# Another order of copies, sums and weights in the seven-product stages of a two-block transformer kernel, its attention queries by halves and a part of its branch products inside the attention's tail

## The reference, cut to what matters

```python
h = _rmsnorm(x, norm1_g[l]) * (1.0 + scale1) + shift1
proj = h @ w_in[l]                                    # 1024 x 4352
qa, ka, va, qd, kd, vd, ga, gd = jnp.split(proj, points, axis=-1)
out_a = _sliding_window_attention(...)                # 8 heads, 512 wide
...
out_d = _diff_attention(...)                          # 4 heads of 128, then an RMS norm
merged = (jax.nn.sigmoid(ga) * (out_a @ w_branch_swa[l])
          + jax.nn.sigmoid(gd) * (out_d @ w_branch_diff[l]))
x = x + gate1 * (merged @ w_out[l])

h2 = _rmsnorm(x, norm2_g[l]) * (1.0 + scale2) + shift2
# _conv_ffn: u = h2 @ w_up (1024 x 5632), split into a and g
a = ap[:, 0:s] * conv_w[0] + ap[:, 1:s + 1] * conv_w[1] + ap[:, 2:s + 2] * conv_w[2] + conv_b
return (jax.nn.gelu(a, approximate=False) * g) @ w_down
```

## Time and profile before

| | before |
|---|---|
| median of 3 runs | 2781.86 us (2779.5 to 2788.24) |
| the profiled execution | 2779.05 us, span 2777.2 us |
| mean granted clock of PE | 0.974 of full speed |
| PE busy | 2594.6 us (93%), 12363 matmuls |
| DVE, ACT, POOL busy | 1548.2, 1110.3, 854.9 us (56, 40, 31%) |
| chain that ended last | PE 75%, DVE 12%, ACT 6%, DMA 4% |
| its largest lines | L1654 28%, L1739 21%, L1808 8% |
| a weight split of POOL, mean | 1030 ns (L1468) and 2431 ns (L1473) |

### The profile page before, as it was taken

One profiled execution on the slowest core, in us unless ns is written; L12 is line 12 of the kernel. 1 busy time (PEld: TensorE's weight loads), 2 busy tenths in 40 slices (PEclk: granted clock), 3 DMA queues, 4 the chain that ended last, 5 costly groups with the idle time before them and its releaser, 6 DMA issues.

```text
span 2777.2 us, 34668 instructions
## 1 busy us (share of the span) xinstructions
PE 2594.6 (93%) x12363; PEld 2157.6 (78%) x12363; DVE 1548.2 (56%) x2099; ACT 1110.3 (40%) x1866; POOL 854.9 (31%) x626
## 2 busy tenths in 40 slices
PE   3899999999999999999899988869997999999998
PEld 2688888788788799987788868757876888887887
DVE  5666665640325466657864428765568777772112
ACT  3400001421401588856544437660255555551000
POOL 1133332012233566620232220233102233225664
PEclk7999999999999999999999999999999999999999
DMA  5244443343266544435253347413242333338933
GB/s 216 80 148 137 137 143 115 100 161 133 84 215 194 141 107 107 107 125 159 91 184 113 116 119 191 175 39 122 76 145 68 114 106 107 118 96 303 294 90 123
DMA packets 375993, 374.81 MB, mean 135 GB/s; under 512 B 36068, under 2 KB 284301, under 8 KB 375693
## 3 DMA queue, kind: packets, MB, share of 16 engines
q1 hardware_dynamic: 345564, 303.90, 36.9%
q10 hardware_dynamic: 30256, 68.69, 6.6%
HBM read 286.55 MB, written 85.98 MB: 134 GB/s over the span
## 4 chain that ended last, share of the span: by engine, by line
PE 75%; DVE 12%; ACT 6%; DMA 4%; issue 1%; POOL 1%; SPq 0%; ACTq 0%; DVEq 0%; POOLq 0%
PE PS L1654 28%; PE PS L1739 21%; PE PS L1808 8%; PE PS L752 5%; PE PS L730 2%; PE PS L1721 2%; PE PS L1698 1%; DMA mod_raw<-in_w_ada 1%; PE PS L716 1%; PE PS L715 1%; DVE opBf L2847 1%; PE PS L1853 1%; ACT opA L1998 1%; ACT opBf L1994 1%; DVE M L2508 1%
## 5 line engine op out<-in xcount | busy, mean ns | idle before, releaser
L1654 PE MATMUL PS<-opA,w_hi 128*128 128x512 f32 x2304 | 722.1, 393 | 19.1 <-POOL w_lo L1473 13.7
L1654 PEld LDWEIGHTS PS<-opA,w_hi 128*128 128x128 f32 x2304 | 435.8, 189 | 113.5 <-POOL w_lo L1473 16.1
L1654 PE MATMUL PS<-opA,w_lo 128*128 128x512 f32 x1152 | 451.0, 391 | 0.0
L1468 POOL CAST w_hi<-w_raw 128x1024 fp32r<-128x1024 f32 (+1 forms) x120 | 123.6, 1030 | 776.1 <-PE PS L1654 467.4
L1739 PE MATMUL PS<-opB,Xr 128*128 128x512 f32 x1120 | 309.7, 394 | 15.0 <-ACT M L2173 15.0
L1473 POOL TENSOR_TENSOR w_lo<-w_raw,w_hi 128x1024 fp32r<-128x1024 f32 (+1 forms) x122 | 296.6, 2431 | 84.5 <-ACT w_hi L2053 74.9
L1739 PE MATMUL PS<-opA,Xr 128*128 128x512 f32 x980 | 278.7, 395 | 6.3 <-DVE M L2864 3.4
L2508 DVE SCALAR_TENSOR_TENSOR M<-mod_raw,small,M 128x512 f32<-128x512 f32 x168 | 176.0, 1048 | 162.3 <-DMA mod_raw<-in_w_ada 82.5
L1739 PEld LDWEIGHTS PS<-opB,Xr 128*128 128x128 f32 x1120 | 212.9, 190 | 61.2 <-ACT M L2173 16.3
L1654 PEld LDWEIGHTS PS<-opA,w_lo 128*128 128x128 f32 x1152 | 218.1, 189 | 45.1 <-issue 0.2
L1739 PEld LDWEIGHTS PS<-opA,Xr 128*128 128x128 f32 x980 | 184.1, 190 | 50.7 <-ACT M L2173 8.4
(11 more groups left out here) (241 smaller groups left out, 4687.8 us busy)
## 6 DMA issues: line engine op xcount, KB each, us to landing
mod_raw<-in_w_ada SPq DMA_DIRECT2D x96, 256.0 KB, 2.9
z_dram<-opB ACTq DMA_DIRECT2D x44, 512.0 KB, 3.9
w_raw<-in_a_w_in SPq DMA_DIRECT2D x32, 512.0 KB, 4.8
hin<-q_dram SPq DMA_DIRECT2D x64, 256.0 KB, 5.9
w_raw<-in_w_down SPq DMA_DIRECT2D x32, 512.0 KB, 4.3
opA<-z_dram SPq DMA_DIRECT2D x60, 256.0 KB, 5.1
mod_raw<-in_b_mod_w SPq DMA_DIRECT2D x48, 256.0 KB, 2.9
X<-x_dram SPq DMA_DIRECT2D x24, 512.0 KB, 7.5
```

Of the source, the lines that this page charges most:

```text
L1468: pool.tensor_copy(hi, raw).then_inc(pool_done, 1)
L1654: ins = pe.matmul(ps, w[:, k0 + k, :], rhs(part, k0 + k), start=(k == 0 and n == 0), stop=(k == chunks - 1 and n == 2))
```

## The change

It changes no arithmetic, and consists of three parts.

1. In the heads of both seven-product stages the first weights' copies come before the second half of the token copies, and the copies and sums come in another order. In the FFN yt gets a second tile (`yt_odd`), so that chunks take turns, and the first chunk's g half is copied out of PSUM (`first_gates`).
2. In the FFN's iterations both halves of chunk i + 1 are handled together, and `z_store` goes to the iteration's end.
3. In the second attention, queries of the first four chunks are loaded by halves of the tokens, the lower ones after P1 of the last in-projection iteration; the weights of branch units 0 and 1 are loaded and split inside the attention, and their 4 chunks that belong to the sliding-window half (48 matmuls) run inside its tail (`branch_swa`); the last norm has its own tile `d_last`, and its square stands one step sooner. Six of sixteen gate tiles are loaded later.

SP's list, for the queries, and PE's, for the branch products:

```diff
+            def query_half(c, e, hf):
+
+                t = slice(hf * HALF, (hf + 1) * HALF)
+                for part in range(2):
+                    sp.dma_start(opA[part * DH:(part + 1) * DH, e, c, t].bitcast(F32),
+                                 q2_dram[part, c * P + e * DH:c * P + (e + 1) * DH, t]).then_inc(q_half[c][hf], 16)
+                    step(q_half[c][hf], "q_half", c, hf, by=16)
...
             sp.wait_ge(in2_stored[1], at("in2_stored", U_IN2 + 17))
+            sp.wait_ge(pe_done, at("seven", U_IN2, LAST_IN2, P1))
+            for c in range(4):
+                for e in range(2):
+                    query_half(c, e, 0)
             sp.wait_ge(pe_done, at("seven", U_IN2, LAST_IN2, P7))
             sp.wait_ge(dve_done, at("seven_w", U_IN2, LAST_IN2, P3))
+            query_half(0, 0, 1)
             swa_keys_values(0)
+            sp.wait_ge(pe_done, at("seven", U_IN2, LAST_IN2, P4))
+            query_half(0, 1, 1)
+            for c in range(1, 4):
+                for e in range(2):
+                    query_half(c, e, 1)
 
             sp.wait_ge(pe_done, at("seven", U_IN2, LAST_IN2, P3))
-            for c in range(4):
-                queries(c)
-                if c == 1:
-                    swa_keys_values(1)
+            swa_keys_values(1)
             for j in range(DIFF_HEADS):
                 queries(4 + j)
             diff_keys(1)
```

```diff
+            def branch_swa(n, hf):
+
+                pe.wait_ge(pool_done, at("split", U_BRANCH + n))
+                if (n, hf) == (0, 0):
+                    pe.wait_ge(dve_done, at("swa_out", 3, 1))
+                    pe.wait_ge(dve_done, at("sec_p", STEPS - 1, 0))
+                for k in range(4):
+                    for m, (w, part) in enumerate(((0, 0), (1, 0), (0, 1))):
+                        pe.matmul(PS[:, 2 * n + hf, :], branch_part(n, w)[:, k, :], opA[:, part, k, hf * HALF:(hf + 1) * HALF],
+                                  start=(k == 0 and m == 0), stop=(k == 3 and m == 2))
+
+
             for t in range(SECOND_STEPS):
                 x = turned_at(t)
+                if x == 0:
+                    pe.wait_ge(dve_done, at("block", U_IN2, LAST_IN2, 0, 1))
+                if t == STEPS:
+                    branch_swa(0, 0)
+                if t == STEPS + DIFF_VALUE:
+                    branch_swa(0, 1)
                 if t < SWA_STEPS:
...
                     values(t)
+            for hf in range(2):
+                branch_swa(1, hf)
 
         def stick_act(act):
```

The loop of the FFN stage, ACT's list and then DVE's:

```diff
             for i in range(1, SEVENS[q]):
                 f = i + 2
                 snap(q, i, 0)
                 weight_high(q, i + 1, P1)
                 weight_high(q, i, P3)
-                gelu(f - 1, 1)
-                z_high(f - 1, 1)
+                if i == 1:
+                    for first in (1, 0):
+                        for hf in range(2):
+                            z_high(first, hf)
+                else:
+                    for hf in range(2):
+                        first_tap(f - 1, hf)
                 weight_high(q, i + 1, P2)
-                first_tap(f, 0)
-                z_store(f - 1)
                 snap(q, i, 1)
+                if i == 1:
+                    for hf in range(2):
+                        first_tap(f - 1, hf)
+                    z_store(0)
+                    z_store(1)
+                for hf in range(2):
+                    gelu(f - 1, hf)
                 weight_high(q, i + 1, P6)
-                gelu(f, 0)
                 weight_high(q, i + 1, P5)
+                if i > 1:
+                    for hf in range(2):
+                        z_high(f - 1, hf)
                 snap(q, i, 2)
                 weight_high(q, i + 1, P7)
                 weight_high(q, i + 1, P4)
-                z_high(f, 0)
-                first_tap(f, 1)
-            gelu(FC - 1, 1)
-            z_high(FC - 1, 1)
+                if i == 1:
+                    for hf in range(2):
+                        z_high(f - 1, hf)
+                z_store(f - 1)
+            for hf in range(2):
```

```diff
+            for i in range(1, SEVENS[q]):
                 f = i + 2
-                if i:
-                    other_taps(f - 1, 1)
-                    weight_low(q, i + 1, P1)
-                    weight_low(q, i, P3)
-                    gated(f - 1, 1)
-                    block_sum(q, i, 0, 0)
-                    z_low(f - 1, 1)
-                    weight_low(q, i + 1, P2)
-                    other_taps(f, 0)
-                    weight_low(q, i + 1, P6)
-                    weight_low(q, i + 1, P5)
-                    block_sum(q, i, 1, 1)
+                weight_low(q, i + 1, P1)
+                weight_low(q, i, P3)
+                for hf in range(2):
+                    other_taps(f - 1, hf)
+                block_sum(q, i, 0, 0)
+                weight_low(q, i + 1, P2)
+                for hf in range(2):
+                    gated(f - 1, hf)
+                weight_low(q, i + 1, P6)
+                weight_low(q, i + 1, P5)
+                for hf in range(2):
+                    z_low(f - 1, hf)
+                block_sum(q, i, 1, 1)
                 weight_low(q, i + 1, P7)
                 block_sum(q, i, 1, 0)
-                gated(f, 0)
                 weight_low(q, i + 1, P4)
```

More of the change, by code:

```diff
@@ L128 @@
 NO_UNIT = range(U_IN2 + 4, U_BRANCH)
+AHEAD = (U_BRANCH, U_BRANCH + 1)
+EARLY_GATES = [n for n in range(2 * KC) if n % KC < KC - 3]
+LATE_GATES = [n for n in range(2 * KC) if n % KC >= KC - 3]
+LAST_HALF = 2 * DIFF_HEADS - 1
 QK = 4
@@ L526, in program @@
         q_in = [sem(f"q_in{c}") for c in range(KC)]
+        q_half = [[sem(f"q_half{c}_{hf}") for hf in range(2)] for c in range(4)]
         k_in, v_in = [[sem(f"k_in{s}_{hf}") for hf in range(2)] for s in range(3)], [sem(f"v_in{s}") for s in range(2)]
@@ L666, in second_loads @@
                 sp.wait_ge(in2_stored[row], at("in2_stored", in2_unit(LAST_IN2, row)))
-            for n in range(2 * KC):
+            for n in range(2):
+                branch_weights(n)
+            for n in EARLY_GATES:
                 sp.dma_start(gates[:, n, :], gate_dram[n]).then_inc(gates_in, 16)
@@ L1027, in second_act @@
                     swa_high(y)
-                if half_at(t, 1) is not None:
-                    square(half_at(t, 1))
+                if squared_at(t) is not None:
+                    square(squared_at(t))
                 if half_at(t, RMS_LAG + 1) is not None:
@@ L1382, in _ @@
                         reload_half_spilled(U_IN2, j)
+                if u == U_BRANCH + 5:
+                    sp.wait_ge(pe_done, at("unit", U_BRANCH + 1, 1))
+                    for n in LATE_GATES:
+                        sp.dma_start(gates[:, n, :], gate_dram[n]).then_inc(gates_late, 16)
+                        step(gates_late, "gates_late", by=16)
                 if u in (U_IN2, U_FFN):
@@ L1639, in _ @@
                     second_pool()
-                if u not in SPLIT_BY_DVE and u not in NO_UNIT:
+                if u not in SPLIT_BY_DVE and u not in NO_UNIT and u not in AHEAD:
                     split(u)
@@ L1703, in quad @@
                                 step(pe_done, "unit", v, hf)
+                        if (first, hf, k) == (0, 1, QK - 1):
+                            ins.then_inc(pe_done, 1)
+                            step(pe_done, "b12_read", u)
                         if (first, hf, k) == (0, 0, 2):
@@ L2355, in first_copies, with first_gates @@
                 names[("free", u)] = names[("fa", f, 1)]
+            def first_gates(u):
+                for hf in range(2):
+                    act.wait_ge(pe_done, at("unit", u, 1))
+                    act.wait_ge(x_half[1], at("x_half", U_FFN, 1))
+                    act.wait_ge(dve_done, at("lo", "n2", 15))
+                    act.wait_ge(act_done, now(act_done))
+                    act.activation(first_gate(hf), PS[:, bank(u, hf), :], ACT.Copy).then_inc(act_done, 1)
+                    step(act_done, "first_gate", hf)
+                names[("free", u)] = names[("first_gate", 1)]
             def gelu(f, hf):
@@ L2360, in gelu @@
                 act.wait_ge(act_done, now(act_done))
[L2361 removed]
+                act.activation(gelu_tile(f, hf), gelu_tile(f, hf), ACT.Gelu).then_inc(act_done, 1)
                 step(act_done, "fg", f, hf)
@@ L3011, in _ @@
             weight_low(q, 0, P5)
+            weight_low(q, 0, P1)
+            weight_low(q, 0, P2)
             token_sums(q, 2)
+            token_sums(q, 3)
             weight_low(q, 0, P7)
             weight_low(q, 0, P3)
-            token_sums(q, 3)
-            weight_low(q, 0, P1)
-            weight_low(q, 0, P2)
+            for which in (P6, P5, P7, P4):
+                for c in range(QK):
+                    token_low(q, which, c)
             for hf in range(2):
                 other_taps(0, hf)
-            for c in range(QK):
-                token_low(q, P6, c)
-            for c in range(QK):
```

(11 more changed lines are left out.)

241 lines of the change are left out of this document (143 added, 98 removed).

## The result

The changed kernel takes 2805.94 us in the median of 4 runs (2801.18 to 2808.57), the kernel before beside it 2780.68. The medians are 25 us apart; the ratio is 1.0084, 95% interval 1.0059 to 1.0109, which makes it 23 us slower. The forecast was 2797, range 2766 to 2814.

The account below looks back on a forecast made before the run. PE, busy 2594.6 of 2777.2 us, was taken to bound the kernel. In-projection head −0.9, attention −23.0, FFN head +0.4, FFN loop +25.5 and clock +14 made +16: median 2797 us, range 2766 to 2814.

Parts of the forecast that it names:

- four taps in 4.2: Sign in the FFN loop: DVE's taps row at about 4.2 us in place of 3.2 for four.
- FFN head: FFN stage up to P1(2): old 11.28 us wait goes, some 14 us forms at P3(1); +0.4 us (−3 to +3).
- attention's start: Second attention up to its first turn: lower query halves asked for earlier shorten PE's 11.58 us idle; −6.7 us (−5 to −9).
- main case: 2.0 us stall at P3 each FFN iteration, clock falling behind about half: +16 us, 2788 to 2806; chance 0.45.
- FFN loop: FFN iterations 2 to 19: P3 waits for DVE's block_sum(1,1); 33.1 us of stalls less 7.6 saved, net +25.5 us.
- the two collisions: FFN loop: POOL sums delay DVE's taps and second z_low on the shared port; stall 2.0 us, a single collision 1.0.
- The clock: FFN loop: PE's clock drops behind half of 17 stalls, 1.7 us each; +14 us (0 to +29).
- The in-projection head: Up to the in-projection's first P3: PE begins sooner but DVE's list holds the same instructions; −0.9 us (−3 to +1.5).
- The splits inside the attention: Two POOL weight splits now stand inside its attention work; +1.5 us (0 to +3).
- The tail: Attention's end: 48 branch matmuls done in PE's waits, weights already split, 336 matmuls left in 76.2 us; −17.8 us.

Follow-up runs that it names:

- pool1: Changed kernel with POOL's weight sum for P5 alone held back until block_sum(1,1) in the FFN loop; 2779.02 us, ratio 0.9987.
- pool2: Changed kernel with POOL's weight sum for P3, and what is queued behind it, held back until block_sum(1,1) in the FFN loop; 2760.66 us, ratio 0.9921.
- head: pool2 with chunk 2's z_lows behind weight_low P4 in FFN iteration 1 alone; 2755.59 us, ratio 0.9900.
- allpieces: head with the branch splits' subtraction in eight pieces and every POOL weight sum of both seven-product stages in four; 2748.11 us, ratio 0.9862.
- keys: Kernel before with the attention's part alone, keys and values asked for ahead of the first two upper query DMAs; 2764.46 us, ratio 0.9936.

## Why the prediction was right, point by point

The mechanism was the forecast one, and its signs came: sixteen waits of nearly 2 us at P3, four taps in 4.2, one wait of 13.84 in the FFN head. One sign failed, on the attention's start. The size was short: 2806 lies at the upper end of the main case's own 2788 to 2806, and that the total isn't further off is in part luck, since errors in the loop had opposite signs.

- **The FFN loop** was the right place with the right price. The block sum was forecast at +17.60 to +18.29 and P3 at +18.34; that is where they are. Stalls: 33.1 us forecast for 17 of them. Measured, counted by P3's late start: 16 x 2.02 + 1.13 = 33.5. Two small things were missing. Iteration 19, which I had at 0, waits 1.30 (1.46 late), since the last chunk's work stands in it too. And each stall makes the twelve matmuls behind it 3.02 long in place of 2.88, 0.14 x 18 = 2.5 us. `pool1` and `pool2` show that the two collisions, not the count of DVE instructions, make the wait; the count costs 0.25 us an iteration.
- **The clock** was charged as half of 17 drops at 1.7, +14. It was 7 at 1.6, +11. The errors (2.5 + 1.5 against 3) cancel in large part, by luck. That drops follow some waits and not others of the same length I could not predict, and no run explains which.
- **The FFN head**: +0.4 forecast, +0.2 measured, with the wait of 13.84 us at P3(1) in place of 11.28 ahead of P6(1). `head` and `allpieces` confirm the reason, a backlog of DVE.
- **The in-projection head**: -0.9 forecast, -0.8 measured.
- **The attention's start** was mis-sized: -6.7 forecast, -3.7 measured (about -4.6 in eight of the eleven other kernels, -2.7 to -6.2 in all). The two waits there make 7.9 us, 3.7 less than the 11.58 of before and not the 5 to 9 less that were to show it. I had the first chunk's last upper query DMA issued at 1652.4. In the changed kernel, where this place lies 5.7 us later, that would be 1658.1. SP's timeline, and the two DMAs of that half (time of an issue in ns, then landing: least, median, most):

```profile
1641.17 11.91 SPq L684 DMA_DIRECT2D opA<-q_dram  x18
1653.12 3.02 SPq L638 DMA_DIRECT2D keys<-k_dram  x4
...
L684 SPq DMA_DIRECT2D opA<-q_dram x2: 969/2716/4463, 1657.6 to 1662.1; - x2
DMA to landing us min/median/max: 5.6/7.3/9.0
```

  The first was issued at 1657.6 and its issue took 4.46 us; so the second was issued only at 1662.1, landed 5.6 later, and PE's second wait ended at 1667.76, 3 us after the forecast place. I had also left out the keys' landing, which holds the first scores to 1663.0; but `keys` shows that their place in the queue doesn't matter, as the second wait takes over. Why that one issue took so long, no run shows.
- **The splits inside the attention** cost 3.2 where +1.5 was taken (range to +3). I priced them as POOL being late; they also hold DVE's short instructions, the same mechanism as in the loop, which I didn't apply there. The time at the lower clock in this stretch differs between executions: it takes 1.9 to 5.2 us more than before in the nine kernels with whole subtractions, and -0.2 to +1.8 in the three with pieces.
- **The tail**: -17.8 forecast, -16.4 measured, and here the forecast was better than this trace shows. In nine of the eleven other kernels the same stretch is 105.3 us in place of 107.0, which is -18.0. The difference is a clock drop at its start; PE has no further wait in it, and the branch row is the forecast one. Windows of the changed kernel and of `head` at the same place (granted clock is the number behind POOL's count), and the changed kernel's chain:

```profile
1855.60:1859.20 3.60, 3.52 (x13) 3.13 (x14) 1.04 (x4) 2.12 (x5) 0.51 (x1) 0.53 0.00 0
```

```profile
1853.00:1856.50 3.50, 3.46 (x28) 3.29 (x28) 1.98 (x6) 2.79 (x6) 0.47 (x1) 1.00 0.00 0
```

```profile
1880.72 76.17 PE PS L1754 x336
```

So +16 was 7 us short of +23, 6 of them in the attention: 3.0 at its start, 1.7 at the splits, 1.4 in a clock drop of the tail.

## What to carry to other kernels

A list that just fits its slot on paper has no room for what another engine takes from it: lay out the shared engine's instructions in time beside it, and count each pair of DVE and POOL instructions that both read two tiles in SBUF. Where such pairs can't be parted in time, cut POOL's instruction into pieces: POOL then takes longer and DVE loses next to nothing. That is a gain where a collision is on the path; where the pair had been parted already, the pieces cost 3.9 us in the loop of `allpieces`. When the profile of a change looks too bad or too good, cut both traces at the same instructions first; here 6 us of the difference lay in code that hadn't changed, and a stretch that loses 1.6 us to a clock drop in one execution doesn't in the next.

## What the runs showed of the hardware

- POOL's sum of 128 x 512 in one instruction beside four taps: POOL 1.30, taps 4.21. In four instructions: POOL 3.14, taps 3.36. DVE's loss falls from 1.03 to 0.18 us, though POOL works longer: the loss went with the length of one instruction of POOL, not with POOL's time in total.
- The Trainium skill, "SBUF — State Buffer", section "Who interferes with whom", calls the port pair that the two engines share an exclusive lock, and says that the order of issue decides who blocks. The trace agrees: POOL's sum at 2206.81 came 0.06 us ahead of the taps and delayed them, and the sum at 2216.02, which came 0.03 behind a low part of DVE, took 1.80 in place of 1.30.
- An idle time in a row is shorter than the delay: P3 started 2.02 us late where the row says 1.86, because the last matmul before it is counted for 0.39 us, where the start of the next one follows after 0.23. With the slower restart (3.02 us for twelve matmuls in place of 2.88) a stall shown as 1.86 costs 2.16, which is what P3 to P3 shows: 21.20 against 19.04.
- The clock fell behind 7 of the 16 waits of 1.86 to 1.88 us, the third or the second after the last in turn (granted clock 0.70 in the window behind one, 1.00 behind another), and behind none of the waits of 0.97 to 1.30.
